# Five arrival slots and three split halves in place of four and four, in a one-core diffusion layer

## The chip, the cores and the metric

The kernel runs on one core of a Trainium2 chip. The metric is the device time of one launch in microseconds. Matrix products run on TensorE (PE), elementwise work on VectorE (DVE), ScalarE (ACT) and GpSimd (POOL); SyncE (SP) issues most of the transfers from memory (HBM).

## What is computed

One layer of a hybrid backbone over 256 latent tokens and 256 context tokens of width 2048, in fp32. Only the latent stream is an output. Cut to what matters:

```python
ul = (xl * (1 + sc1_l) + sh1_l) @ w_in          # combined projection, 2048 -> many columns
uc = (xc * (1 + sc1_c) + sh1_c) @ w_in
ya_c, ya_l = _hgrn_mixer(uc, ul, lb_fwd, lb_bwd, hgrn_norm, need_ctx)   # gated recurrence, two directions
yc_c, yc_l = _attention_mixer(uc, ul, attn_sink, need_ctx)
yb_l = _pool_mixer(ul, pool_w, pool_scale)
xl = _layer_norm(ALPHA * xl + g1_l * _merge_branches(ul, (ya_l, yb_l, yc_l), w_branch, w_out), ln1_g, ln1_b)
xl = _layer_norm(ALPHA * xl + g2_l * _sq_relu_mlp(xl * (1 + sc2_l) + sh2_l, w_ff1, w_ff2), ln2_g, ln2_b)
```

The shifts, scales and gates (`sh1`, `sc1`, `g1`, ...) come from `silu(c) @ w_ada + b_ada`. All weights together are some 370 chunks of 1 MB.

## The kernel before

**Chunks and slots.** Every weight is read in chunks of 512 input rows by 512 columns, as [128, 4, 512] fp32, 1 MB. `stream()` lists them in the order of use. SyncE issues one transfer per chunk into a ring of slots `raw0`, `raw1`, ...: eight slots while the first `w_ada` chunks are read (four of them, the `EXTRA` ones, lie in room that later tiles take), then `RAW` = 4. Before a transfer into a slot it waits until the chunk that held the slot is used up (L373 to L378): for a weight chunk until its second half has its low part (`lo_made`), for a summed chunk until its sum is done (`ada_used`).

**Split halves.** A product in fp32 is made of three matmuls: the weights are split into a high part `whi` (ScalarE's cast, L399) and a low part `wlo` (VectorE's subtraction, L842), the activations likewise, and TensorE adds hi*hi, hi*lo and lo*hi. One half chunk (two of the four row tiles) is split at a time. `whi` and `wlo` have four places, used in turn: half q goes to place q % 4, and ScalarE waits, before it casts half q, until TensorE has finished with half q-4 (L396 to L398; `w_used` and `blk_done` count TensorE's ends). VectorE waits for the cast (`hi_made`), TensorE for the low part (`lo_made`).

**Order by hand.** Each engine has its own program, written out in order. On ScalarE and VectorE the loops over chunks all have one form: `split_after(name, n)` converts both halves of the chunk after n, and then comes the engine's other work of this step, which TensorE wants after its matmuls of chunk n:

- vals, L431 to L455 and L914 on: keys and values; per weight chunk VectorE also sums two `w_ada` chunks (`ada_sum`, L856 to L864, four steps for a chunk).
- forget, four groups of four chunks: one sum per chunk, and a gate block (L926 to L953) of four scans and logs, whose keys ScalarE makes (L473) and TensorE turns at the end of the group (L1437).
- mix, two groups of twelve chunks: nine levels of the recurrence. GpSimd makes the exponents (L720 to L723), ScalarE the exponentials (L536), VectorE copies the scores of level k-1 (L988, L990) and multiplies the operands of the next (`lv`, L975), and TensorE makes the scores (L1483) after the chunk; then the outputs (L1494 to L1497).
- gates, branch 0: sixteen attention units. After each chunk TensorE makes one unit's scores (L1529) and turns another's probabilities (L1537). VectorE does a unit's mask, maximum and scaling (L1065 to L1078) behind the split.
- gates, branches 1 and 2, then the output projection (`out`), and the MLP in four parts of 16 + 16 chunks (`mlp`).

`features` (L1253 to L1255) keeps weights as the stationary operand and gives columns x tokens; a half is 24 matmuls of 256 or 512 columns. `tokens` (L1292 to L1294) gives tokens x columns for two tiles of 128 tokens (t = 0, 1); a half is 12 matmuls of 512 columns. For the last block of `out` and of `mlp` the last two chunks (`apart=2`) are gone through for tile 0 first and then for tile 1, so that tile 0's row work (`out_rows`, or `ff_out` and `last_rows`) begins while TensorE works on tile 1. All four places are held in this stretch.

Of the kernel before, what the change touches and what calls it, by code (L numbers as in the profile page):

```python
# [7 lines left out]
F32 = mybir.dt.float32  # L8
F32R = mybir.dt.float32r
# [5 lines left out]
P = 128  # L15
# [4 lines left out]
PW = 512  # L20
# [8 lines left out]
NEG = -1e30  # L29
WINDOWS = (2, 4, 8, 16)  # L30
LEVELS = (128, 64, 32, 16, 8, 4, 2, 1, 0)
RAW = 4

EXTRA = 4


PAN_AQ, PAN_AI, PAN_AG, PAN_AF, PAN_B, PAN_CQ, PAN_CKV, PAN_GATE = 0, 2, 4, 6, 10, 12, 14, 15
# [52 lines left out]
def stream():  # L90
# [14 lines left out]

    st.ring = RAW
    done = 0
# [96 lines left out]
PN = panels()  # L204


def build(nc, vecs, cst, rcnt, masks, xT, xtok, rows, w_ada, w_in, pool_w, w_br, w_out, w_f1, w_f2, outT):
    weights_of = {"w_ada": w_ada, "w_in": w_in, "w_br": w_br, "w_out": w_out, "w_f1": w_f1, "w_f2": w_f2}
    with ExitStack() as ctx:
        KB = 1024  # L210
# [4 lines left out]
        def at(name, shape, off, dt=F32):  # L215
            return nc.alloc_sbuf_tensor_at(name, shape, dt, offset=base + int(off))

        slots = [at(f"raw{n}", [P, CK, PW], off * KB)
                 for n, off in enumerate((0, 8, 16, 24, 160, 168, 184, 208))]
        whi = at("whi", [P, 4, 2, PW], 32 * KB, F32R)  # L220
        wlo = at("wlo", [P, 4, 2, PW], 48 * KB, F32R)

# [92 lines left out]
        hi_made, lo_made, ada_used, raw_used = sem("hi_made"), sem("lo_made"), sem("ada_used"), sem("raw_used")  # L317
# [69 lines left out]
        def _(act):  # L387
# [3 lines left out]
            def split(name, n, halves=(0, 1)):  # L391
                slot = ST.slot(name, n)
                act.wait_ge(raw_full[slot], ST.full(name, n))
                for h in halves:
                    q = ST.half(name, n, h)
                    if q >= 4:  # L396
                        which, count = PN.last[q - 4]
                        act.wait_ge(ended[which], count)  # L398
                    nc.scalar.copy(whi[:, q % 4], slots[slot][:, 2 * h:2 * h + 2]).then_inc(hi_made, 1)  # L399

            def split_after(name, n):
                if ST.following(name, n):
# [430 lines left out]
        def _(dve):  # L833
            TT, TS, STT = nc.vector.tensor_tensor, nc.vector.tensor_scalar, nc.vector.scalar_tensor_tensor
            drain = nc.vector.drain

            def split(name, n, halves=(0, 1)):
                slot = ST.slot(name, n)
                for h in halves:
                    q = ST.half(name, n, h)  # L840
                    dve.wait_ge(hi_made, q + 1)
                    TT(wlo[:, q % 4], slots[slot][:, 2 * h:2 * h + 2], whi[:, q % 4].bitcast(F32),  # L842
                       ALU.subtract).then_inc(lo_made, 1)

            def split_after(name, n):
# [393 lines left out]
        def _(pe):  # L1239
# [7 lines left out]
            def half_ready(name, n, h):  # L1247
                q = ST.half(name, n, h)
                pe.wait_ge(lo_made, q + 1)
                return q % 4  # L1250

            def three(out, w_hi, w_lo, x_hi, x_lo, start, stop):
                mm(out, w_hi, x_hi, start=start, stop=False)  # L1253
# [344 lines left out]

            for i in range(4):
                tokens("out", 4 * i, 4, 2 * (i % 2), mR, ready=lambda k: pe.wait_ge(m_lo, k + 1),  # L1600
                       between=lambda k: merged(3) if i == 0 and k == 0 else None, apart=2 if i == 3 else 0)

            def normalized(q, t):

# [14 lines left out]
            for f in range(4):  # L1619
                for i in range(4):  # L1620
                    def after(k):
                        if f == 0 and i == 0 and k < 2:
                            normalized(2 + k, 0)
                            normalized(2 + k, 1)
                    features("mlp", 32 * f + 4 * i, h2, 0, T, ready=lambda k, h: pe.wait_ge(h2_lo, 2 * k + h + 1),
                             between=after)
                for i in range(4):
                    tokens("mlp", 32 * f + 16 + 4 * i, 4, 2 * (i % 2), hid,
                           ready=lambda k: pe.wait_ge(hid_lo, 16 * f + 4 * k + 4),
                           between=lambda k: ada_spread(12 + f) if i == 0 and k == 0 else None,  # L1630
                           apart=2 if f == i == 3 else 0)


def constants():
# [65 lines left out]
```

## Time and profile before

| | us |
|---|---|
| median of 3 runs | 2015.3 |
| lowest, highest | 2012.96, 2015.35 |
| profiled execution, its own time | 2018.67 |
| its span | 2016.9 |
| TensorE busy | 1905.7 |
| VectorE busy | 1267.5 |
| ScalarE busy | 784.7 |
| GpSimd busy | 439.9 |

The mean granted clock of TensorE is 0.976 of full speed, and 409 MB move at a mean of 203 GB/s. Times inside the span are counted from its start. A row of the timeline gives start, length, engine, line, operation, tiles, a count of merged equal instructions, and in brackets the engine's idle time before it and what ended it. TensorE's matmuls overlap, so a matmul's own length is more than its share of the time.

### The profile page before, as it was taken

To read this page: it belongs to the slowest core of one execution; us is meant where nothing else is said; L and a number is where in the kernel's file an instruction comes from. 1 tells how busy PE (TensorE), PEld (TensorE's weight loads), DVE (VectorE), ACT (ScalarE), POOL (GpSimd) and SP (SyncE) were. 2 spreads that over 40 slices of the span, in tenths; PEclk is the share of its full clock that TensorE was granted. 3 is DMA by queue.
4 is the path that set the end of the run, shared out by engine and by line. 5 is a ranking of instruction groups with operands and counts; after the bars stand their busy time and mean duration, and the time that the engine had idled before them with its cause. 6 is when DMAs were issued, how large, how long until landed. Compare 5 with 4: busy or idle time off the path is not lost.

```text
span 2016.9 us, 26285 instructions
## 1 busy us (share of the span) xinstructions
PE 1905.7 (94%) x10808; PEld 1634.5 (81%) x10808; DVE 1267.5 (63%) x1419; ACT 784.7 (39%) x898; POOL 439.9 (22%) x335
## 2 busy tenths in 40 slices
PE   6899899999898989999999999999999999999996
PEld 1478787889888867777778887997899899889975
DVE  1345656785666575667867666767566556556686
ACT  1221224454544545544344444533333333333332
POOL 0000000003727322023421000246045005302510
PEclk8999999999999999999999999899999999999998
DMA  9956554454333244456666674465665556656552
GB/s 401 421 199 225 215 197 175 169 188 168 105 126 111 98 159 144 147 173 265 229 234 248 263 257 167 185 242 179 229 230 218 200 209 223 212 192 225 217 180 89
DMA packets 59320, 409.05 MB, mean 203 GB/s; under 512 B 6336, under 2 KB 9024, under 8 KB 10304
## 3 DMA queue, kind: packets, MB, share of 16 engines
q1 hardware_dynamic: 54720, 395.34, 53.4%
q10 hardware_dynamic: 4480, 12.02, 1.6%
q8 instruction: 86, 1.41, 0.3%
q14 instruction: 34, 0.28, 0.0%
HBM read 405.24 MB, written 2.10 MB: 202 GB/s over the span
## 4 chain that ended last, share of the span: by engine, by line
PE 71%; DVE 13%; DMA 4%; DVEq 3%; issue 3%; POOL 3%; ACT 2%; POOLq 0%; SPq 0%; ACTq 0%
PE main L1292 12%; PE main L1294 12%; PE main L1293 12%; PE main L1253 9%; PE main L1254 9%; PE main L1255 9%; DVE asum L863 5%; DVE wlo L842 4%; DMA raw<-in_w_in 2%; DVEq L862 2%; DMA raw<-in_w_ada 2%; PE side L1324 1%; ACT whi L399 1%; PE side L1483 1%; PE main L1343 1%
## 5 line engine op out<-in xcount | busy, mean ns | idle before, releaser
L842 DVE TENSOR_TENSOR wlo<-raw,whi 128x1024 fp32r<-128x1024 f32 x552 | 742.4, 1372 | 414.3 <-ACT whi L399 413.8
L399 ACT CAST whi<-raw 128x1024 fp32r<-128x1024 f32 x552 | 571.8, 1050 | 854.6 <-PE main L1294 349.1
L1253 PE MATMUL main<-h,whi 128*128 128x256 f32 x1024 | 291.4, 285 | 4.1 <-DVE h L1160 2.1
L1254 PE MATMUL main<-h,whi 128*128 128x256 f32 x1024 | 291.0, 284 | 0.0
L1255 PE MATMUL main<-h,wlo 128*128 128x256 f32 x1024 | 290.9, 284 | 0.0
L1253 PE MATMUL main<-hCL,whi 128*128 128x256 f32 (+1 forms) x800 | 264.6, 331 | 14.0 <-DVE wlo L842 3.8
L1254 PE MATMUL main<-hCL,whi 128*128 128x256 f32 (+1 forms) x800 | 260.5, 326 | 0.0
L1255 PE MATMUL main<-hCL,wlo 128*128 128x256 f32 (+1 forms) x800 | 260.2, 325 | 0.0
L863 DVE SCALAR_TENSOR_TENSOR asum<-raw,sm,asum 128x512 f32<-128x512 f32 x240 | 200.9, 837 | 19.7 <-issue 0.9
L1292 PE MATMUL main<-whi,hid 128*128 128x512 f32 x512 | 201.9, 394 | 5.1 <-DVE wlo L842 4.4
L1253 PEld LDWEIGHTS main<-h,whi 128*128 128x128 f32 x1024 | 197.9, 193 | 4.8 <-DVE h L1160 2.5
L1293 PE MATMUL main<-wlo,hid 128*128 128x512 f32 x512 | 200.0, 391 | 0.0
L1294 PE MATMUL main<-whi,hid 128*128 128x512 f32 x512 | 199.9, 390 | 0.0
L1254 PEld LDWEIGHTS main<-h,whi 128*128 128x128 f32 x1024 | 197.8, 193 | 0.1
L1255 PEld LDWEIGHTS main<-h,wlo 128*128 128x128 f32 x1024 | 197.8, 193 | 0.0
L823 POOL TENSOR_TENSOR sq<-sq 128x256 f32<-128x256 f32 x64 | 66.2, 1035 | 521.1 <-DVE sq L1169 513.4
L1253 PEld LDWEIGHTS main<-hCL,whi 128*128 128x128 f32 x800 | 155.3, 194 | 27.3 <-DVE wlo L842 10.8
L1255 PEld LDWEIGHTS main<-hCL,wlo 128*128 128x128 f32 x800 | 154.7, 193 | 11.9
L1254 PEld LDWEIGHTS main<-hCL,whi 128*128 128x128 f32 x800 | 155.0, 194 | 11.4 <-issue 0.2
L1292 PE MATMUL main<-whi,hCL 128*128 128x512 f32 x384 | 155.6, 405 | 8.8 <-DVE wlo L842 8.8
L1293 PE MATMUL main<-wlo,hCL 128*128 128x512 f32 x384 | 150.7, 393 | 0.0
L1294 PE MATMUL main<-whi,hCL 128*128 128x512 f32 x384 | 150.7, 392 | 0.0
(229 smaller groups left out, 2674.3 us busy)
## 6 DMA issues: line engine op xcount, KB each, us to landing
raw<-in_w_f SPq DMA_DIRECT2D x128, 1024.0 KB, 5.0
raw<-in_w_in SPq DMA_DIRECT2D x108, 1024.0 KB, 5.0
raw<-in_w_ada SPq DMA_DIRECT2D x96, 1024.0 KB, 7.0
raw<-in_w_br SPq DMA_DIRECT2D x24, 1024.0 KB, 6.9
raw<-in_w_out SPq DMA_DIRECT2D x16, 1024.0 KB, 5.0
xin<-in_xT SPq DMA_DIRECT2D x4, 1024.0 KB, 19.9
ax<-in_xtok ACTq DMA_DIRECT2D x1, 2048.0 KB, 8.0
lng<-in_rows ACTq DMA_DIRECT2D x2, 1024.0 KB, 5.8
```

The costliest lines, as they stand in the source:

```text
L399: nc.scalar.copy(whi[:, q % 4], slots[slot][:, 2 * h:2 * h + 2]).then_inc(hi_made, 1)
L823: TT(sq[:, b], sq[:, b], sq[:, b], ALU.mult)
L842: TT(wlo[:, q % 4], slots[slot][:, 2 * h:2 * h + 2], whi[:, q % 4].bitcast(F32), ALU.subtract).then_inc(lo_made, 1)
L862: drain()
L863: last = STT(asum[:], slots[slot][:, j], s, asum[:], ALU.mult, ALU.add)
L1253: mm(out, w_hi, x_hi, start=start, stop=False)
L1254: mm(out, w_hi, x_lo, start=False, stop=False)
L1255: return mm(out, w_lo, x_hi, start=False, stop=stop)
L1292: mm(out, x[:, kt, 0, own], whi[:, par, j], start=start, stop=False)
L1293: mm(out, x[:, kt, 0, own], wlo[:, par, j], start=False, stop=False)
L1294: last = mm(out, x[:, kt, 1, own], whi[:, par, j], start=False, stop=stop)
L1324: last = mm(side[group, 1 + p % 2], sR[:, k * CK + j], slots[slot][:, j], start=k == 0, stop=k == 3, tile_position=(0, 32 * j), skip_group ...
```

## The change

The ring has five slots after the first stage in place of four; the early stage has eight in both (5 + 3). The split halves have three places in place of four, so ScalarE's cast of half q waits for TensorE's end of half q-3. The fifth slot takes the 8 KB that the two fourth places gave up. The last block of `out` and of `mlp` keeps one chunk apart in place of two.

```diff
-RAW = 4
-
-EXTRA = 4
+RAW = 5
+
+HALVES = 3
+
+EXTRA = 3
...
         slots = [at(f"raw{n}", [P, CK, PW], off * KB)
-                 for n, off in enumerate((0, 8, 16, 24, 160, 168, 184, 208))]
-        whi = at("whi", [P, 4, 2, PW], 32 * KB, F32R)
-        wlo = at("wlo", [P, 4, 2, PW], 48 * KB, F32R)
+                 for n, off in enumerate((0, 8, 16, 24, 32, 160, 168, 184))]
+        whi = at("whi", [P, HALVES, 2, PW], 40 * KB, F32R)
+        wlo = at("wlo", [P, HALVES, 2, PW], 52 * KB, F32R)
...
                     q = ST.half(name, n, h)
-                    if q >= 4:
-                        which, count = PN.last[q - 4]
+                    if q >= HALVES:
+                        which, count = PN.last[q - HALVES]
                         act.wait_ge(ended[which], count)
-                    nc.scalar.copy(whi[:, q % 4], slots[slot][:, 2 * h:2 * h + 2]).then_inc(hi_made, 1)
+                    nc.scalar.copy(whi[:, q % HALVES], slots[slot][:, 2 * h:2 * h + 2]).then_inc(hi_made, 1)
...
-                    TT(wlo[:, q % 4], slots[slot][:, 2 * h:2 * h + 2], whi[:, q % 4].bitcast(F32),
+                    TT(wlo[:, q % HALVES], slots[slot][:, 2 * h:2 * h + 2], whi[:, q % HALVES].bitcast(F32),
...
-                return q % 4
+                return q % HALVES
...
-                       between=lambda k: merged(3) if i == 0 and k == 0 else None, apart=2 if i == 3 else 0)
+                       between=lambda k: merged(3) if i == 0 and k == 0 else None, apart=1 if i == 3 else 0)
...
-                           apart=2 if f == i == 3 else 0)
+                           apart=1 if f == i == 3 else 0)
```

What this moves in the engines' programs. SyncE, in the stage of keys and values, where two `w_ada` chunks stand between two `w_in` chunks; in brackets is the count that the transfer waits for. Before:

```order
47 L379 DMA raw2_51<-in_w_in 128x2048 [waits ada_used]
48 L379 DMA raw3_52<-in_w_ada 128x2048 [waits lo_made]
49 L379 DMA raw0_49<-in_w_ada 128x2048 [waits ada_used]
50 L379 DMA raw1_50<-in_w_in 128x2048 [waits ada_used]
51 L379 DMA raw2_51<-in_w_ada 128x2048 [waits lo_made]
```

And of the changed kernel, the same five transfers:

```order
47 L381 DMA raw2_51<-in_w_in 128x2048 [waits ada_used]
48 L381 DMA raw3_52<-in_w_ada 128x2048 [waits ada_used]
49 L381 DMA raw4_53<-in_w_ada 128x2048 [waits lo_made]
50 L381 DMA raw0_49<-in_w_in 128x2048 [waits ada_used]
51 L381 DMA raw1_50<-in_w_ada 128x2048 [waits ada_used]
```

The order of the transfers is the same, but a `w_in` chunk now takes the slot of the first of the two sums before it, and the wait for the second sum (`ada_used`) has moved to the `w_ada` chunk behind it.

TensorE, in the last four half chunks of the MLP, the first matmul of each run of six (one half, one tile); `hid_lo` marks where the last chunk is begun for tile 0. Before:

```order
9939 L1292 MATMUL main<-whi_57,hid_89 128x512 [waits lo_made]
...
9945 L1292 MATMUL main<-whi_57,hid_89 128x512 [waits lo_made,hid_lo]
...
9951 L1292 MATMUL main<-whi_57,hid_89 128x512 [waits lo_made]
...
9957 L1292 MATMUL main<-whi_57,hid_89 128x512 [waits lo_made]
...
9963 L1292 MATMUL main<-whi_57,hid_89 128x512 [waits lo_made]
```

And of the changed kernel:

```order
9939 L1294 MATMUL main<-whi_57,hid_89 128x512 [waits lo_made]
...
9945 L1294 MATMUL main<-whi_57,hid_89 128x512 [waits lo_made]
...
9951 L1294 MATMUL main<-whi_57,hid_89 128x512 [waits lo_made]
...
9957 L1294 MATMUL main<-whi_57,hid_89 128x512 [waits lo_made,hid_lo]
...
9963 L1294 MATMUL main<-whi_57,hid_89 128x512 [waits lo_made]
```

Before, tile 0 enters the last chunk two runs earlier and is done with it at row 9956, ahead of four runs for tile 1; now it is done at row 9968, ahead of two. The order of ScalarE's, VectorE's and GpSimd's instructions is unchanged; what the casts wait for is not.

## Rows read from the trace of the kernel before

**Rows 1.** The page, shares of the chain that ended last, by engine.

```profile
PE 71%; DVE 13%; DMA 4%; DVEq 3%; issue 3%; POOL 3%; ACT 2%; POOLq 0%; SPq 0%; ACTq 0%
```

**Rows 2.** TensorE's waits, whole span: waiting line <- releaser: us, times, longest.

```profile
PE side L1483 <- DVE lv L975: 18.8, 10, 3.5
...
PE side L1437 <- ACT kctx L473: 4.4, 3, 2.6
```

**Rows 3.** ScalarE's waits, whole span.

```profile
ACT whi L399 <- PE main L1294: 349.1, 213, 6.0
ACT whi L399 <- PE main L1255: 303.7, 156, 9.4
ACT whi L399 <- DMA raw<-in_w_in: 192.1, 31, 13.1
```

**Rows 4.** Stretches: length, busy PE, PEld, DVE, ACT, POOL, then clock, DMA share, GB/s.

```profile
173.00:251.00 78.00, 67.67 (x368) 58.69 (x368) 46.17 (x56) 17.78 (x22) 0.00 (x0) 0.91 0.58 213
...
480.00:694.00 214.00, 191.01 (x1463) 185.72 (x1462) 135.18 (x125) 99.46 (x95) 105.80 (x66) 0.96 0.35 121
694.00:887.00 193.00, 183.79 (x809) 145.30 (x809) 122.78 (x182) 102.72 (x151) 44.36 (x20) 0.97 0.41 139
```

**Rows 5.** Timeline of ScalarE where keys and values are projected.

```profile
173.44 1.99 ACT L399 CAST whi<-raw 128x1024 fp32r<-128x1024 f32 x2 [12.66 <-DMA raw<-in_w_in]
...
188.39 2.01 ACT L399 CAST whi<-raw 128x1024 fp32r<-128x1024 f32 x2 [11.01 <-DMA raw<-in_w_in]
```

**Rows 6.** Timelines of ScalarE, VectorE and TensorE around one attention unit.

```profile
751.46 1.05 ACT L399 CAST whi<-raw 128x1024 fp32r<-128x1024 f32 x1 [1.62 <-PE main L1294]
...
752.14 2.35 DVE L842 TENSOR_TENSOR wlo<-raw,whi 128x1024 fp32r<-128x1024 f32 x2
...
755.31 0.69 DVE L1068 TENSOR_REDUCE col<-side 128x1 f32<-128x512 f32 x1 [0.43 <-issue]
...
758.02 0.49 DVE L1078 TENSOR_SCALAR pr<-pr,col 128x512 f32<-128x512 f32 x1
...
758.04 1.02 PE L1529 MATMUL side<-ak,qr 128*128 128x512 f32 x2
758.90 0.60 PE L1537 MATMUL side<-cs,pr 128*128 128x128 f32 x4
```

**Rows 7.** Timelines of ScalarE, VectorE and TensorE among the recurrence levels.

```profile
569.10 1.04 ACT L399 CAST whi<-raw 128x1024 fp32r<-128x1024 f32 x1 [1.78 <-PE main L1255]
...
487.74 1.22 DVE L975 TENSOR_TENSOR lv<-lv,q_t 128x1024 f32<-128x1024 f32 x1
...
519.65 3.44 DVE L842 TENSOR_TENSOR wlo<-raw,whi 128x1024 fp32r<-128x1024 f32 x2 [1.38 <-ACT whi L399]
...
524.46 2.11 DVE L975 TENSOR_TENSOR lv<-lv,q_t 128x1024 f32<-128x1024 f32 x1
...
526.62 2.05 PE L1483 MATMUL side<-lv 128*128 128x128 f32 x16 [0.48 <-DVE lv L975]
```

**Rows 8.** Timelines of ScalarE, VectorE and TensorE around one turn of the keys.

```profile
356.30 1.06 ACT L399 CAST whi<-raw 128x1024 fp32r<-128x1024 f32 x1 [1.29 <-PE main L1255]
...
367.18 1.06 ACT L399 CAST whi<-raw 128x1024 fp32r<-128x1024 f32 x1 [2.92 <-PE main L1255]
...
368.68 2.35 DVE L842 TENSOR_TENSOR wlo<-raw,whi 128x1024 fp32r<-128x1024 f32 x2
371.13 3.24 DVE L863 SCALAR_TENSOR_TENSOR asum<-raw,sm,asum 128x512 f32<-128x512 f32 x4
...
378.55 1.10 PE L1437 MATMUL side<-cs,kctx 128*128 128x128 f32 x8 [0.53 <-ACT kctx L473]
```

**Rows 9.** TensorE's waits between 870 and 1170 us.

```profile
PE main L1292 <- DVE wlo L842: 8.8, 7, 2.5
```

**Rows 10.** Timeline of VectorE at the end, the first rows of either token tile.

```profile
1994.97 0.69 DVE L1180 TENSOR_TENSOR res<-main,g2b 128x512 f32<-128x512 f32 x1 [3.20 <-PE main L1294]
...
2004.68 0.68 DVE L1180 TENSOR_TENSOR res<-main,g2b 128x512 f32<-128x512 f32 x1
```

## The prediction

> **What bounds the kernel now.** I read the chain that ended last first: TensorE's own work is 71% of the span, VectorE's 13%, DMA 4% [rows 1]. So TensorE sets the time, and everything else costs only what TensorE waits for. Then I read TensorE's waits by releaser. The largest group is the level scores of the recurrence, released by VectorE's `lv` product, 18.8 us; the turned keys are 4.4 us [rows 2], and between 870 and 1170 us the low parts `wlo` of the weights are 8.8 us [rows 9]. Third, ScalarE's waits: it sat idle before the cast `whi` for 349.1 and 303.7 us until TensorE had finished with a half chunk, and for 192.1 us until a chunk had landed [rows 3]. These two kinds of wait are what the change moves: it buys arrival room (a fifth slot) with conversion room (a fourth half). Neither kind of wait is on the path by itself. The question is at each place what is queued behind it. Last I read the stages: in 173 to 251 us TensorE is idle 78 - 67.7 = 10.3 us at a clock of 0.91, in 480 to 694 us 23.0 us at 0.96, in 694 to 887 us 9.2 us at 0.97 [rows 4].
>
> **The fifth slot.** It pays where two `w_ada` chunks are summed per weight chunk. There the casts start at 173.44 and 188.39 us, both the moment a chunk lands, and so on at this pace for five chunks [rows 5]. One turn is 14.95 us: transfer, two casts, two `wlo`, two sums, and only then the next transfer's slot is free. In the new order of SyncE a weight chunk waits for the first sum, not for the second. A sum of one chunk is 3.24 us [rows 8], so the turn falls to 11.7 us. TensorE's 67.7 us of work for the five chunks of this stretch, at a clock of 0.91 [rows 4], are 67.7 x 0.91 / 5 = 12.3 us a chunk at full speed, so TensorE sets the pace again. What goes is the 10.3 us of idle time and, with the waits, most of what the low clock costs, 78 x 0.09 = 7 us at most. Gain: 15 us, between 8 and 17. Elsewhere ScalarE's waits for a landing are not followed by a wait of TensorE of any size, so I give the slot nothing more.
>
> **The missing half.** Cast q now waits for TensorE's end of half q-3 instead of q-4. ScalarE and VectorE always convert both halves of the following chunk ahead of their other work. With four halves, the second half of chunk k+1 was cast when chunk k began. Now it is cast when the first half of chunk k ends, one half later. Where VectorE has nothing to do but this, it is free: a cast is 1.05 us, a `wlo` 2.35 / 2 = 1.2 us, with hand-overs 2.4 us from the release to the ready pair, and TensorE comes two halves later, over 5.2 us (the time between two releases of ScalarE, its idle time and the cast before it, is TensorE's half: 1.62 + 1.05 = 2.67 us with tokens [rows 6], 1.78 + 1.04 = 2.82 us with 256 columns [rows 7]). That covers the MLP and the output projection. Where work that TensorE needs at the end of chunk k stands behind this `wlo`, it is not covered. Three stages have that form.
>
> *Attention*, 16 units. Behind the `wlo` pair stand the mask, maximum, exponential's sum and scaling of a unit: pair 752.14 to 754.49, scaling done at 758.02 + 0.49 = 758.51, so 4.0 us after the pair, 3.6 us without this unit's own pause of 0.43 us; TensorE turns the result at 758.90 [rows 6]. New: the pair ready 2.4 us after the release, then 3.6 us and a hand-over, 6.1 us after the first half's end. TensorE has 2.67 us of matmuls and 758.90 - 758.04 = 0.86 us of the next scores in that time. It waits 2.6 us per unit, and 3.4 us in the last two of eight, which have no scores to issue. That is 2 x (6 x 2.6 + 2 x 3.4) = 45 us; about 5 of the 9.2 us idle there now [rows 4] are the same waits. Cost 40 us. Bounds: 30, if in some units VectorE is late anyway and the cast's lateness costs nothing, and 50, with the pause in each.
>
> *Recurrence levels*, 18. Behind the pair (519.65 to 523.09) stand two copies and the product of the next level, done at 524.46 + 2.11 = 526.57; TensorE starts at 526.62 [rows 7], 3.5 us after the pair. The same product takes 1.22 us elsewhere [rows 7], so 2.6 us is the other end. New: 2.4 + 2.6 to 3.5 us after the first half's end, against 2.82 us of matmuls: 2.2 to 3.1 us per level, 2.6 taken. The first level of each group has no copies (0.8 us), and the inter-chunk output behind it has two exponentials and two products (about 3.7 us). That is 2 x (0.8 + 8 x 2.6 + 3.7) = 50.6 us, in place of today's 18.8 us [rows 2], since a level that waits for the split is no longer waiting for GpSimd. Cost 32 us, bounds 22 and 40.
>
> *Forget gates*, three turns of keys. The second cast was released at 367.18, VectorE took its pair at 368.68 to 371.03, and TensorE got the keys at 378.55, 7.5 us later, behind a sum and a gate block [rows 8]. One half of 512 columns is (367.18 - 356.30) / 2 = 5.4 us. In the new order the release is one half later, at 372.6; the pair ends at 374.95 and the keys come at 382.5: 3.9 us later. TensorE's matmuls end 0.53 us before the keys come today, so it would wait 4.4 us. Three turns of 4.4 us against 4.4 us in all today [rows 2]: cost 9 us, between 6 and 11.
>
> *Second branch*, 887 to 1031 us. Here `wlo` ends just as TensorE needs it (8.8 us of waits [rows 9]), behind a sum. At three places the later cast pushes the pair by 2 us: cost 6 us, between 0 and 10.
>
> **Ends apart.** The last token block lets its first 128 tokens finish early. With one chunk apart in place of two, the first tile ends one half's time later, 2.67 us. VectorE's work on it begins at 1994.97 and runs without a gap into the second tile's at 2004.68 [rows 10], so VectorE is the path there and the end moves by all of it: 2.7 us. At the output projection the same happens ahead of the norm: 2.7 us. A few places of the MLP (residual rows on VectorE and GpSimd) add 4 us, between 0 and 6. Cost 9.4 us.
>
> **The clock.** Each wait costs more than itself: the granted clock is 0.91, 0.96 and 0.97 in the three stretches [rows 4], short spells at 1.2 GHz around the longer waits. Time lost so is at most 78 x 0.09 = 7 us on 10.3 us of idle time, 214 x 0.04 = 9 us on 23.0 us, 193 x 0.03 = 6 us on 9.2 us, so 0.4 to 0.7 us per us idle; a part of a spell falls into the wait itself and costs nothing. The terms above add 87 us of waits and take 10 away. I take 0.35 of 77, 27 us, between 0 and 0.6 of it, 46 us.
>
> **Sum.** -15 + 40 + 32 + 9 + 6 + 9.4 + 27 = +108 us. The profiled execution took 2018.7 us and the median is 2015.3 us; both contain the same waits, so I add it to the median: 2124 us.
>
> **A rule weighed.** The rows show TensorE two halves away from the half that ScalarE casts, and VectorE with 4 us of other work in between. The Trainium skill (Trainium Kernel Development and Optimization, Best Practices) asks to double-buffer so that transfers overlap compute. By that rule three halves, and five slots, are plenty: only the gain in transfers and the two tails would be seen, which is the first rival.
>
> **Rivals.** (1) *Faster: the cover holds.* If ScalarE's and VectorE's lateness stays inside the conversion room, only the slot's gain and the ends remain: -15 + 5.4, about 2006 us. It decides if what stands behind the pair is under 0.3 us (2.7 - 2.4). The rows show 4.0, 3.5 and 7.5 us [rows 6 to 8], and TensorE already starts within 0.4 us of VectorE in the first two. Chance 0.03. (2) *The waits come, the clock stays.* 2015.3 + 81 = 2097 us. For it speaks that most new waits are under 3 us; against it that the attention now loses 6 us of clock on waits of the same size. Chance 0.22. (3) *The clock falls behind nearly every new wait, and `wlo` collides more with GpSimd*: 2150 us and more, chance 0.13. (4) *The slot does nothing*, because the third sum's transfer queues ahead of the weight chunk: +15 us, 2140 us, chance 0.05. (5) Gains and losses cancel: 0.02. The forecast itself has 0.55.
>
> **Numbers.** 2124 us; the range 2088 to 2160 takes in rival 2 and most of rival 3. About 0.2% is what a measurement can tell from no change: faster 0.03, same 0.02, slower 0.95.
>
> **What would show it.** TensorE's waits for `lv` near 50 us, for `pr` or the attention's products near 45 us, for `kctx` near 13 us; waits in 173 to 235 us gone and ScalarE's casts there every 11.5 us; ScalarE's wait for a landing under 192.1 us; granted clock under 0.95 in 480 to 900 us; the last part of the page's busy row unchanged but 2.7 us longer. I am wrong if the level scores still wait under 25 us, or if the casts of second halves are released by TensorE without its waiting afterwards.

## The result

The changed kernel took 2142.9 us (median of four runs, 2140.2 to 2149.5), against 2015.3 for the kernel before; the ratio is 1.0605, 95% interval 1.0568 to 1.0642. In a later group of runs the same two kernels gave 2146.4 and 2018.4, ratio 1.0621 (1.0591 to 1.0652). The change makes the kernel slower by 6%. Ratios leave out one execution, in the run with the shorter distance alone, that took 6614.3 us. In the code of the changed kernel everything behind the first edit stands two lines lower: L1483 is now L1485, L1529 is L1531, L842 is L844, and so on; in the experiments the rows have each run's own line numbers, and the tile names tell which line is meant.

**The path.** Of the changed kernel, the page's shares of the chain that ended last [before: rows 1]:

```profile
PE 77%; DVE 11%; issue 4%; ACT 4%; DMA 2%; DVEq 1%; POOL 1%; POOLq 0%; ACTq 0%; SPq 0%
```

TensorE still sets the time, and has the same 10808 matmuls. The span rose from 2016.9 to 2142.5 us. It must be looked for in what TensorE waits for, and in the rate at which it works.

**TensorE's waits**, whole span of the changed kernel (waiting line, releaser, us, times, longest), to be held against [rows 2] and [rows 9]:

```profile
PE side L1485 <- DVE lv L977: 37.9, 16, 3.7
PE side L1531 <- ACT col L591: 28.5, 12, 2.7
...
PE side L1539 <- DVE pr L1080: 16.5, 4, 6.4
PE side L1439 <- ACT kctx L475: 13.5, 3, 4.6
PE side L1531 <- POOL ak L758: 6.5, 1, 6.5
PE side L1496 <- issue: 6.5, 2, 3.2
PE side L1485 <- DVE lv L979: 4.1, 2, 2.1
```

The level scores wait 37.9 + 4.1 us where it was 18.8, the keys 13.5 where it was 4.4, and the attention (scores L1531, transposes L1539) waits 28.5 + 16.5 + 6.5 = 51.5 us in 17 places, where the kernel before waited 9.2 us in three. ScalarE's waits, beside [rows 3]:

```profile
ACT whi L401 <- PE main L1296: 545.9, 269, 9.2
ACT whi L401 <- PE main L1257: 506.7, 190, 13.8
ACT whi L401 <- DMA raw<-in_w_in: 68.7, 8, 9.8
```

This is the exchange in three rows: ScalarE waits 123 us less for chunks to land (192.1 to 68.7) and 400 us more for TensorE to give a place back (349.1 + 303.7 to 1052.6).

**Stretches** of the changed kernel, columns as in [rows 4]: the start, the late part of keys and values, forget and query, the recurrence (482 to 742), the attention (742 to 985), the second branch.

```profile
0.00:173.00 173.00, 145.80 (x710) 88.38 (x711) 63.18 (x102) 38.11 (x52) 1.66 (x6) 0.93 0.85 340
173.00:251.00 78.00, 78.00 (x447) 68.75 (x446) 50.47 (x61) 18.53 (x20) 0.00 (x0) 1.00 0.71 257
...
300.00:480.00 180.00, 164.17 (x916) 145.19 (x915) 113.73 (x174) 76.18 (x110) 5.09 (x4) 0.93 0.44 158
...
482.00:742.00 260.00, 211.38 (x1509) 203.67 (x1510) 121.26 (x130) 103.32 (x97) 94.70 (x70) 0.91 0.29 98
742.00:985.00 243.00, 191.53 (x740) 144.05 (x739) 112.45 (x177) 96.72 (x147) 33.38 (x17) 0.90 0.33 111
...
985.00:1170.00 185.00, 170.34 (x720) 137.62 (x719) 132.69 (x109) 68.85 (x75) 63.59 (x35) 0.97 0.61 228
```

And of the kernel before, its recurrence (480 to 699) and its attention (699 to 882), the same work as in the fourth and fifth row above:

```profile
480.00:699.00 219.00, 196.01 (x1505) 190.72 (x1504) 136.32 (x128) 104.11 (x100) 107.01 (x67) 0.96 0.34 118
699.00:882.00 183.00, 173.79 (x746) 136.16 (x745) 116.64 (x178) 96.09 (x144) 38.41 (x18) 0.97 0.43 147
```

The second row shows the gain: in 173 to 251 us TensorE has no idle time at all and the full clock, where it had 10.3 us and 0.91 [rows 4]. The fourth and fifth row show the loss: 49 and 51 us without work where it was 23 and 9, and a clock of 0.91 and 0.90 where it was 0.96 and 0.97.

Taken by the end of the last half of each stage, the difference to before is (us; a stage's own length, after minus before):

| stage | length before | difference |
|---|---|---|
| up to the eighth values chunk | 173.2 | +0.4 |
| values 8 to forget 1 | 87.4 | -17.8 |
| forget 2 to 15 | 165.3 | +9.4 |
| query | 53.8 | +10.1 |
| recurrence levels | 219.7 | +40.3 |
| attention | 182.5 | +61.0 |
| second branch | 140.1 | +9.6 |
| third branch and projection | 235.0 | -0.7 |
| MLP, first quarter | 201.5 | +6.9 |
| MLP, the rest | 541.8 | +3.8 |
| behind TensorE's last half | 16.6 | +2.7 |

The differences add up to 125.7, the spans differ by 125.6. TensorE's idle gaps of over 0.25 us are 94.2 us in all before and 176.5 after, 82 us more. The mean clock of 0.976 over 2016.9 us is 48 us of lost time, 0.958 over 2142.5 us is 90: 42 us more. These two make up the loss. The mean clock counts low spells inside the waits too, so as a check without it: the same 10808 matmuls keep TensorE busy for 1946.3 us in place of 1905.7, 40.6 us more, and it is without work for 196.2 us in place of 111.2, the end behind its last half included.

**One attention unit** of the changed kernel, timelines of ScalarE, VectorE and TensorE [before: rows 6]:

```profile
788.17 1.05 ACT L401 CAST whi<-raw 128x1024 fp32r<-128x1024 f32 x1 [1.18 <-PE main L1296]
...
792.20 0.69 ACT L588 ACTIVATE pr<-side,col 128x512 f32<-128x512 f32 x1 [1.19 <-DVE col L1074]
...
789.26 1.23 DVE L844 TENSOR_TENSOR wlo<-raw,whi 128x1024 fp32r<-128x1024 f32 x1 [1.01 <-ACT whi L401]
790.58 0.30 DVE L1067 TENSOR_TENSOR side<-side,cs 128x128 f32<-128x128 f32 x1
...
772.67 1.84 PE L1531 MATMUL side<-ak,qr 128*128 128x512 f32 x2 [2.25 <-ACT col L591]
...
790.24 0.39 PE L1295 MATMUL main<-wlo,yR 128*128 128x512 f32 x1
...
793.21 1.91 PE L1531 MATMUL side<-ak,qr 128*128 128x512 f32 x2 [2.36 <-ACT col L591]
```

To be read in this order: the cast of the second half cannot begin before 788.17, when TensorE has ended the first half of the running chunk. VectorE stands idle 1.01 us for it, makes the low part, and only at 790.58 turns to the mask and the maximum of a unit whose scores have lain ready for 16 us: in step k VectorE works on unit k-2, and this unit's scores were made at 772.67 and done at 774.5. TensorE's own matmuls end at about 790.85. The exponential (792.20) is 1.6 us behind the mask. TensorE's next scores go into the bank that this exponential reads, so it goes on at 793.21, after 2.36 us. Such a wait of 2.35 or 2.36 us stands ten times in the stage.

### The profile page after: what moved, and what is told of

Read it like the earlier page. It is cut to its first block, busy times and chain, and to the rows that moved or that the text cites. A ratio compares the mean times of both kernels' runs of the same rounds, so it can differ in the third digit from the quotient of the medians.

```text
span 2142.5 us, 26285 instructions
## 1 busy us (share of the span) xinstructions
PE 1946.3 (91%) x10808; PEld 1661.1 (78%) x10808; DVE 1237.6 (58%) x1419; ACT 788.3 (37%) x898; POOL 418.9 (20%) x335
## 3 DMA queue, kind: packets, MB, share of 16 engines
q1 hardware_dynamic: 54720, 395.34, 50.6%
## 4 chain that ended last, share of the span: by engine, by line
PE 77%; DVE 11%; issue 4%; ACT 4%; DMA 2%; DVEq 1%; POOL 1%; POOLq 0%; ACTq 0%; SPq 0%
PE main L1294 11%; PE main L1295 11%; PE main L1296 11%; PE main L1255 10%; PE main L1256 10%; PE main L1257 10%; DVE wlo L844 4%; ACT whi L401 2%; PE side L1485 2%; DMA raw<-in_w_ada 2%; DVE asum L865 2%; PE main L1345 2%; PE main L1347 1%; PE main L1346 1%; PE side L1326 1%
## 5 line engine op out<-in xcount | busy, mean ns | idle before, releaser
L844 DVE TENSOR_TENSOR wlo<-raw,whi 128x1024 fp32r<-128x1024 f32 x552 | 734.8, 1340 | 728.4 <-ACT whi L401 728.2
L401 ACT CAST whi<-raw 128x1024 fp32r<-128x1024 f32 x552 | 578.6, 1051 | 1135.1 <-PE main L1296 545.9
L865 DVE SCALAR_TENSOR_TENSOR asum<-raw,sm,asum 128x512 f32<-128x512 f32 x240 | 195.3, 814 | 19.7 <-issue 0.9
L1294 PE MATMUL main<-whi,hCL 128*128 128x512 f32 x384 | 159.4, 415 | 14.7 <-DVE wlo L844 14.7
L1255 PEld LDWEIGHTS main<-hCL,whi 128*128 128x128 f32 x800 | 157.7, 197 | 14.5 <-DVE wlo L844 2.7
L1256 PEld LDWEIGHTS main<-hCL,whi 128*128 128x128 f32 x800 | 157.0, 196 | 11.4 <-issue 0.2
L1296 PE MATMUL main<-whi,hCL 128*128 128x512 f32 x384 | 153.0, 398 | 0.0
L825 POOL TENSOR_TENSOR sq<-sq 128x256 f32<-128x256 f32 x64 | 40.1, 626 | 535.9 <-DVE sq L1171 528.2
```

The source lines that it names most:

```text
L401: nc.scalar.copy(whi[:, q % HALVES], slots[slot][:, 2 * h:2 * h + 2]).then_inc(hi_made, 1)
L825: TT(sq[:, b], sq[:, b], sq[:, b], ALU.mult)
L844: TT(wlo[:, q % HALVES], slots[slot][:, 2 * h:2 * h + 2], whi[:, q % HALVES].bitcast(F32), ALU.subtract).then_inc(lo_made, 1)
L865: last = STT(asum[:], slots[slot][:, j], s, asum[:], ALU.mult, ALU.add)
L1256: mm(out, w_hi, x_lo, start=False, stop=False)
L1294: mm(out, x[:, kt, 0, own], whi[:, par, j], start=start, stop=False)
```

## The experiments

Times in brackets are those of the kernel before in the same group of runs.

### The ring set back to four slots

```diff
-RAW = 5
+RAW = 4
-EXTRA = 3
+EXTRA = 4
```

> The changed kernel with the ring of arriving chunks set back to four slots (and the fourth slot for the MLP stages kept, so that four are extra in place of three). Three halves and the shorter distance at the end stay. Theory: the fifth slot alone ended the loading waits of 11 us in the values stage, so they come back between 173 and 260 us, and no other stage changes: the stretch from the fifth values chunk to the second forget chunk is 17 to 18 us longer again, the span 2158 to 2161. Rival (the slot did nothing; the loading waits went for another reason, because conversions now sit nearer to the arrivals): the time stays at 2143 within 2, and no wait of 11 us at the first matmul of a half comes back.

2171.5 us (2017.3), ratio 1.0762 (1.0738 to 1.0786). The window and the casts of this kernel:

```profile
173.00:251.00 78.00, 67.03 (x364) 58.02 (x362) 43.74 (x55) 15.15 (x19) 0.00 (x0) 0.91 0.58 209
...
181.39 1.99 ACT L401 CAST whi<-raw 128x1024 fp32r<-128x1024 f32 x2 [12.66 <-DMA raw<-in_w_in]
196.21 2.00 ACT L401 CAST whi<-raw 128x1024 fp32r<-128x1024 f32 x2 [10.88 <-DMA raw<-in_w_in]
```

The idle 11 us, the clock of 0.91 and the casts 14.8 us apart are back, as in [rows 4] and [rows 5]. The stretch from values 8 to forget 1 is 88.0 us long, against 69.5 with five slots and 87.4 before; all later stages agree with the changed kernel within 1.1 us. So the slot is worth its 18 us even with three halves, and nothing elsewhere. The time rose by more, 25 to 29 us, and the span is 2167.7 where I had written 2158 to 2161: up to the eighth values chunk the profiled execution of this kernel took 180.9 us, 7.3 more than that of the changed one. The last experiment shows how much this start scatters. But all four executions of this kernel lie between 2169.5 and 2172.0 us, and only one was profiled, so that the whole excess is chance isn't shown.

### The shorter distance alone

```diff
-  apart=2 if i == 3 else 0)          # last block of the output projection
+  apart=1 if i == 3 else 0)
-  apart=2 if f == i == 3 else 0)     # last block of the MLP
+  apart=1 if f == i == 3 else 0)
```

> The kernel before with one edit: the last token tiles of the second projection stage and of the MLP end apart over one chunk, not two. Four slots and four halves stay. Theory: the last tile's last eight matmuls of 256 columns (0.17 us each) no longer lie behind tile 3's own finish, so VectorE's last reductions begin later at both places: 2.7 at the end of the kernel, about 2.7 at the join before the MLP, so 2020 to 2021. The same after VectorE's last reduction (19 us of tail in place of 16.6) should show. Rival (the distance matters only with three halves): 2015 within 1.

2024.8 us (2017.3), the median of all twelve executions, 2023.3 without the long one; ratio 1.0035 (1.0019 to 1.0051), so 4 to 10 us more; I had written 2020 to 2021. The reason that I had given does not fit the code: no matmul of 256 columns is in question, and no row has 0.17 us for one; the edit moves two runs of six matmuls of 512 columns, one half's time. By stages (of the profiled execution, the longest of the other eleven, which also lost 5.2 us in the start): +3.2 in the MLP's first features, +3.0 in its first tokens, +2.7 behind TensorE's last half. VectorE's first row of either tile at the end, beside [rows 10]:

```profile
2008.77 0.69 DVE L1180 TENSOR_TENSOR res<-main,g2b 128x512 f32<-128x512 f32 x1 [5.92 <-PE main L1294]
...
2018.47 0.68 DVE L1180 TENSOR_TENSOR res<-main,g2b 128x512 f32<-128x512 f32 x1
```

TensorE's last half ended at 2011.4, so the second tile's row work began 7.1 us behind it; in the kernel before it was 2004.68 against 2000.3, 4.4 us. Both ends cost what a half costs. The 3.0 us in the MLP's first tokens I had not expected. TensorE waits there for a `wlo` that GpSimd holds up. First two stretches of the kernel before, then the same two, 8 us later, of this one:

```profile
1392.00:1398.00 6.00, 4.61 (x12) 3.16 (x12) 6.00 (x4) 0.56 (x1) 5.16 (x1) 0.72 0.53 175
1398.00:1406.00 8.00, 7.61 (x34) 6.34 (x35) 5.66 (x6) 2.59 (x3) 0.00 (x0) 1.00 0.69 261
```

```profile
1400.00:1406.00 6.00, 3.04 (x12) 2.17 (x12) 6.00 (x4) 1.04 (x1) 5.30 (x1) 0.99 0.51 175
1406.00:1414.00 8.00, 7.47 (x20) 5.93 (x21) 4.63 (x5) 1.05 (x1) 0.00 (x0) 0.58 0.68 251
```

Before, the low clock (0.72) fell on twelve matmuls behind which TensorE waited for VectorE anyway, and cost nothing. Here the same twelve ran at 0.99, TensorE waited longer, and the low clock (0.58) fell on the work after the wait: 8 x 0.42 = 3.4 us of lost time. Why it fell later by this much I can't say. Three halves and a distance of two could not be tried together, since the distance of two holds four halves at once.

### The second conversion behind the attention's work

```diff
 # ScalarE and VectorE, attention stage, step k
-split_after("gates", 12 * h + k)               # both halves of the next chunk
+split_after("gates", 12 * h + k, (0,))         # its first half
 ...                                            # the unit's softmax work
+split_after("gates", 12 * h + k, (1,))         # its second half
```

> The changed kernel (three halves), with one move in the attention stage alone: ScalarE and VectorE convert the first half of the next chunk ahead of the unit's softmax work, as now, but the second half behind it. Theory: the waits of TensorE at the scores, at the transposes and at the rotated keys are there because the softmax work is queued behind a conversion that waits for TensorE to finish a half; with that conversion behind, the stage (705 to 985 in the changed kernel) gives back its 61 us, or all but some 6 to 10: the kernel 2143 to 2085 or 2093, the clock about 0.97, and 28.5 us of score waits and 16.5 of transpose waits fall below 10 together. The recurrence levels, 40 us, stay as they are. Rival A (three halves are too few whatever the order: conversions are late themselves): the score waits go, but waits of the same length stand at the first matmul of a half, and the time stays above 2130. Rival B (the stage is slow for the clock, not for the waits): waits go and low clock stays, 2110 to 2120.

2077.4 us (2017.3), ratio 1.0299 (1.0270 to 1.0328): 65 to 69 us less than with the change alone. The attention's two halves are -1.6 and -0.1 us against before, so all of the 61 us is back, with three halves; I had expected 2085 or more. The waits that are left there, and the stretch of this kernel's attention:

```profile
PE side L1533 <- POOL ak L759: 5.7, 1, 5.7
...
PE side L1541 <- DVE pr L1081: 2.5, 1, 2.5
...
PE side L1533 <- ACT col L591: 1.0, 2, 0.8
...
747.00:927.00 180.00, 170.75 (x740) 133.50 (x739) 114.90 (x176) 97.25 (x146) 37.80 (x18) 0.98 0.44 149
```

28.5 us of score waits are 1.0, 16.5 of transpose waits are 2.5, and the clock went from 0.90 to 0.98 with them. Rival A is out: no waits at first matmuls took their place. The recurrence kept its +40.2.

### The same in the other stages

```diff
 # forget, query, levels: as above; on ScalarE's levels only at k == 10
-split_after("mix", 12 * i + k)
+split_after("mix", 12 * i + k, (0,) if k == 10 else (0, 1))     # ScalarE
-split_after("mix", 12 * i + k)
+split_after("mix", 12 * i + k, (0,))                            # VectorE
 ...                                                             # operands of level k
+split_after("mix", 12 * i + k, (1,))
```

> The changed kernel with the move of the attention run carried to the other stages with work behind the conversions: in forget, query, the recurrence levels (mix) and attention, the second half of the next chunk is converted behind the stage's own work on VectorE, and on ScalarE too except in the first levels, where only the place ahead of the outputs is moved. Theory: all waits but the last 7 of the gates stage came from the order of the queues, so forget gives back 9, query some 8 of 10, and mix some 38 of 40; with attention's 61: from 2143 to 2024 to 2032; waits at the levels (37.9) fall below 20 and at the keys (13.5) below 5. Rival A (three halves are short by themselves in mix, where TensorE's chunks are short): the level waits turn into waits at first matmuls of a half, mix stays 20 or more longer than before, 2045 to 2060. Rival B (the level's work on ScalarE, not VectorE, is late): the mix stage stays at +40, about 2060.

2005.5 us (2018.4), ratio 0.9940 (0.9917 to 0.9963). That is 18.5 us better than the best value I had written, and faster than the kernel before, with three halves; the slot's 17.8 us are in it. Forget is -0.1 us against before, query 0.0, the recurrence -12.9, the attention -1.7, the second branch still +3.6, the MLP +11.1.

```profile
PE side L1493 <- DVE lv L983: 4.7, 8, 1.1
...
460.00:667.00 207.00, 192.21 (x1510) 186.50 (x1511) 135.11 (x130) 103.99 (x98) 109.79 (x70) 0.98 0.36 123
```

The row to look at is the first: it was 37.9 in the changed kernel and 18.8 in the kernel before. I had counted on the state of before as the floor; but of the 18.8 us that stood there some 14 came from the same queue. In the levels VectorE's order is enough: ScalarE still casts both halves ahead there.

### Only VectorE's order, in the attention

```diff
 # VectorE only; ScalarE converts both halves ahead, as in the changed kernel
-split_after("gates", 12 * h + k)
+split_after("gates", 12 * h + k, (0,))
 ...
+split_after("gates", 12 * h + k, (1,))
```

> The changed kernel with the move of the attention run on VectorE alone: there the second half's correction comes behind the unit's softmax work, while ScalarE keeps both conversions ahead of it. Theory: the scores wait for ScalarE, whose softmax steps are queued behind a conversion that waits for TensorE's last half, so VectorE's order gives back little: TensorE's waits at the scores stay within 5 of 28.5, the attention stage stays 45 to 65 longer than before, and the time is 2130 to 2150. VectorE's corrections may come late now and add a few us. Rival (VectorE's correction of the second half was what held up the softmax, as it does the recurrence levels): the stage falls to within 20 of before and the time to about 2100.

2096.6 us (2018.6), ratio 1.0398 (1.0364 to 1.0433). My theory fell and the rival held: the stage is +15.0 us against before, not +45 to +65.

```profile
PE side L1540 <- DVE pr L1080: 9.3, 4, 6.4
...
PE side L1532 <- ACT col L591: 4.3, 5, 1.2
```

I had read the releaser of the long row, ScalarE's `col`, as the cause. It is only the last link: ScalarE's exponential waits for the maximum (`DVE col L1074` in the unit's timeline above), and it was VectorE that stood behind the conversion. Its order alone gives back 46 of the 61 us. With ScalarE's too, as in the run above, it is 63, 1.7 us better than before. ScalarE's order alone can't be tried: its exponential would wait for a maximum that VectorE makes behind the second half, and that half's cast would stand behind the exponential.

### The clock by itself

```diff
+if u >= 3:
+    pe.wait_ge(at_cp, h * 8 + u - 2)
+    for _ in range(16):
+        mm(side[:, 2, 0:T], hCL[:, 0, 0, C:C + P], hCL[:, 0, 0, C:], start=True, stop=True)
 if u >= 2:
     pe.wait_ge(at_exp, h * 8 + u - 1)          # and then the scores
```

> The changed kernel with 16 matmuls of 256 columns added ahead of each wait for the scores in attention (units 3 to 7 of each half), into a bank of the side accumulators that is free there; nobody reads what they write. They fill most of a wait of 2.35 (16 x 0.107 is 1.7) and make nothing that is waited for earlier or later, so they measure the clock's part by itself. Theory: of attention's 61 some 43 is waits and some 20 is TensorE at the lower clock behind them; filled waits leave no low clock behind the scores, the stage (742 to 985) falls by 10 to 15 and the kernel to 2128 to 2133; granted clock of 705 to 985 goes from 0.90 to about 0.95. Rival (the clock falls whatever TensorE does between, or the low clock lies inside waits): the stage keeps its length or grows by up to 17, the clock stays at 0.90.

2134.0 us (2018.4), ratio 1.0586 (1.0556 to 1.0617), beside 1.0621 for the changed kernel in the same group; 1 us above what I had expected, and the intervals overlap, so the stages must speak. TensorE's timeline around one unit, its score waits, and the attention's stretch:

```profile
785.64 2.07 PE L1532 MATMUL side<-hCL 128*128 128x256 f32 x16
788.16 1.12 PE L1535 MATMUL side<-ak,qr 128*128 128x512 f32 x2 [0.44 <-ACT col L591]
...
PE side L1535 <- ACT col L591: 9.5, 12, 2.4
...
742.00:985.00 243.00, 207.68 (x926) 163.37 (x924) 121.41 (x178) 97.44 (x146) 43.13 (x22) 0.94 0.34 115
```

The two stretches of 50 us in which all filled waits lie, of this kernel and then of the changed one:

```profile
775.00:825.00 50.00, 47.43 (x242) 37.86 (x241) 23.84 (x47) 20.23 (x36) 0.00 (x0) 1.00 0.40 137
889.00:939.00 50.00, 47.77 (x243) 38.12 (x243) 23.37 (x47) 21.35 (x36) 0.00 (x0) 1.00 0.32 106
```

```profile
780.00:830.00 50.00, 38.04 (x142) 27.53 (x141) 21.87 (x43) 19.10 (x35) 0.00 (x0) 0.90 0.37 123
900.00:950.00 50.00, 38.22 (x151) 27.65 (x150) 22.95 (x46) 19.82 (x34) 0.00 (x0) 0.94 0.31 106
```

A wait of 2.36 us is now 2.07 us of matmuls and 0.44 us of wait, so nothing moves but the clock. The attention is 8.4 us shorter (I had expected 10 to 15), its clock 0.94 in place of 0.90. TensorE does more work in the stage and finishes it sooner. In the whole stage TensorE's clock fell twelve times in the changed kernel and six times here, never at a filled wait. That is direct evidence that the clock is a price of its own. Ten waits were filled, nine of them of 2.35 or 2.36 us and one of 2.68; 2.07 + 0.44 is 0.15 us more than 2.36, so the matmuls added 1.5 us and the clock gave back 8.4 + 1.5 = 9.9, or 0.4 us for each of the 23.9 us of wait. The five waits at transposes and rotated keys, most of them longer, and the first two at scores were not filled. The rest of the run's gain, 5.5 us in the recurrence, is no effect of the edit, which lies behind it; there the clock came out better for a reason that no run shows. The run with only VectorE's order has the same 4 us less in the first group of the recurrence.

### The slot alone

```diff
+    st.names = (0, 1, 2, 3, 8)       # from the fifth values chunk; slot 8 lies on bytes still unused
 for n in range(16):
+    if n == 2:
+        st.names = (0, 1, 2, 3)      # from the third forget chunk, as before
     panel("forget", n, 0, "w_in", 4 * PAN_AF + n)
```

Four halves and the distance of two stay.

> The kernel before, with the fifth slot alone: four halves and the old distance at the end stay, and the fifth slot lies on bytes that hold nothing yet between the fifth values chunk and the second forget chunk; from there on the ring has four slots again. Theory: the gain of the slot (17.8 us between 173 and 260) stands by itself and needs none of the other parts; its loading waits of 11 us go, all later stages are as before: 1997 to 2000, ratio 0.991 to 0.993. Rival (the gain in that stretch of the changed kernel came with three halves, not with the slot): 2015 within 2. Second rival (the loads that come sooner make the ring empty later, at the switch back to four): some 4 to 8 of the gain stands again as waits in the forget stage, 2004 to 2010.

2000.4 us (2017.3), ratio 0.9920 (0.9896 to 0.9944): faster than the kernel before. Its window is that of the changed kernel:

```profile
173.00:251.00 78.00, 78.00 (x447) 68.75 (x446) 52.71 (x65) 20.19 (x23) 0.00 (x0) 1.00 0.68 247
```

Values 8 to forget 1 is -17.8 us, the same as in the changed kernel to a tenth, and no later stage gives any of it back. The slot pays within these 70 us. It holds its 8 KB for 111 us, from the first transfer into it (issued at 114.3) to the end of its last sum (225.3), while the bytes of a later tile lie idle.

### The slot and the order, with four halves

The edits of "The slot alone" and of "The same in the other stages" on the kernel before.

> The kernel before (four halves, four slots from the second forget chunk on, distance two) with the fifth slot in the early stages, as in the run with the slot alone, and the same moves of the second half's conversion in forget, query, mix and attention. Theory: with four halves half of the waits at the levels (18.7), at the keys (4.4) and at the scores and rotated keys (7) are left from the same queues, so part of them goes with their clock: 1985 to 1995 where the slot alone gave 2000. Rival (with four halves the conversion ahead does not wait for TensorE there, so its place behind only makes the next chunk's halves later): 2000 or above, with new waits at first matmuls of a half.

1979.8 us (2018.4), ratio 0.9811 (0.9786 to 0.9836), the best of all and 5 us below what I had written. Its waits at the levels, and its recurrence:

```profile
PE side L1493 <- DVE lv L983: 4.8, 4, 1.6
...
471.00:673.00 202.00, 189.99 (x1512) 185.47 (x1511) 132.02 (x129) 105.20 (x101) 104.71 (x67) 0.99 0.38 129
```

18.2 us less in the recurrence than before and 8.1 less in the attention, of which the run with the slot alone, whose order there is the old one, already has 3.2. With the order right, the fourth half is still worth something: the run with three halves in the same order loses 5.3 us to this one in the recurrence, 6.4 in the attention, 2.7 in the second branch and some 14 in the MLP and at the end, where the shorter distance is part of it.

### The changed kernel again

> The changed kernel itself again, unaltered, as the yardstick of this group of runs: 2143, and the stages before 173 us tell how much a run's start scatters (the first eight chunks ended between 173.2 and 181.0 in kernels that do the same thing up to there).

2146.4 us (2018.4). From the eighth values chunk on every stage agrees with the first profile within 0.2 us. Only the start differs, 181.2 against 173.7 us. Its first stretch, beside the first row of the stretches of the changed kernel:

```profile
0.00:173.00 173.00, 145.94 (x677) 86.96 (x678) 58.58 (x97) 34.46 (x47) 1.66 (x6) 0.85 0.80 323
```

TensorE is busy for the same 146 us, but at a clock of 0.85 in place of 0.93, and does 677 matmuls in place of 710. Over the whole stage it is without work for 27.2 and 27.1 us, and busy for 146.5 and 154.2. So what scatters from one execution to the next (over all kernels this stage ended between 171.3 and 182.5 us, with 26.9 to 29.4 us without work) is the clock in the start, not the waits for weights. Why the clock differs there, no run shows. In the profiled execution of the run with four slots the 7.3 us are of this kind: 5.1 of them are busy time.

## Why the prediction was right, and where it was not

The forecast was 2124.0 us, the range 2088 to 2160, and the time 2142.9. The direction, the mechanism and the stages were right; the time lies 19 us above the forecast, and rival 4 (2140 us), which came out nearest by its number, is refuted by the runs on the slot.

- **The fifth slot**: -15 predicted, -17.8 measured, the upper bound of 17 just passed. The reading was right: the turn of 14.95 us is gone, and TensorE, busy for all of 173 to 251 us, sets the pace. That pace I had put too slow, at 12.3 us a chunk, by sharing 78 us among five chunks where 5.2 turns fit; and the gain was reckoned for 78 us of a stage of 87.4. Six chunks now take 69.5 us, 11.6 each, and the casts came at 179.69, 190.98 and 202.75 us, every 11.5, as ScalarE's timeline of the changed kernel shows:

```profile
179.69 2.00 ACT L401 CAST whi<-raw 128x1024 fp32r<-128x1024 f32 x2 [5.41 <-DMA raw<-in_w_in]
190.98 2.00 ACT L401 CAST whi<-raw 128x1024 fp32r<-128x1024 f32 x2 [9.30 <-DMA raw<-in_w_in]
202.75 2.00 ACT L401 CAST whi<-raw 128x1024 fp32r<-128x1024 f32 x2 [9.77 <-DMA raw<-in_w_in]
```

Both runs on the slot give the same 18 us.
- **Attention**: the place was right, the waiting row one matmul off. I expected TensorE at the turned probabilities; it stands before the scores, which wait for the exponential of the unit before and come first in its program. The waits are 28.5 + 16.5 + 6.5 = 51.5 us where 45 were predicted, 2.36 us per unit where I had 2.6, and 3.35 us in three of the four last units where I had 3.4. The difference is in the first half: a wait of 6.5 us for GpSimd's rotated keys, which I had not listed, and 6.4 us in place of 3.4 in the seventh unit.
- **Recurrence levels**: 50.6 us of waits predicted, 37.9 + 4.1 + 6.5 = 48.5 found. Single waits lie between 2.0 and 3.7 us, but for one of 0.7, predicted 2.2 to 3.1.
- **Keys**: three waits of 4.4 us predicted, 13.5 us in three found. Forget and query together are 19.5 us longer, where the term was 9: I had not listed a wait of 2.1 us for `q_t` in query, and the clock's share, 0.93 in 300 to 480 us, was far above what 0.35 per us of wait gives.
- **Second branch**: +6 predicted, +9.6 measured, of which 6.1 is idle time; the rest is the clock (0.97 where it was 0.99).
- **Ends**: 9.4 predicted. 2.7 at the end was exact, 3.7 at the join stands for 2.7, and the MLP's 4 us became 7.0 (3.2 in its first tokens, 3.8 later). The run with the distance alone shows that most of the first part belongs to the distance, not to the missing half.
- **The clock**: the step that failed in size. Sum of the waits: 87 less 10 predicted, and 6.7 us of the ends that TensorE waits out, 84 in all; 82 found. The clock's own loss was put at 27 us, less some 5 that leave with the slot, 22 us net, and is 42 (48 to 90 us over the span; 40.6 by the busy time). My own rows said 0.4 to 0.7 us for each us idle; I took 0.35, with the argument that a part of each low spell falls into the wait. What was found is 42 / 82 = 0.51. The run with filled waits gives 0.4 for waits of 2.4 us. Taking the middle of my rows, 0.55 x 77 = 42, would have put the forecast at 2139.
- **The rule weighed**: the Trainium skill (Trainium Kernel Development and Optimization, Best Practices) asks to double-buffer so that DMA overlaps compute. Read as a rule for the halves too, it would call three plenty: some 2006 us, and the kernel took 2142.9. With the second conversion behind the other work it took 2005.5. That the two numbers meet is luck: recurrence and attention came out 14.6 us below the kernel before, the second branch and the MLP 14.7 above it. Three halves cost little where nothing that TensorE needs is queued behind the conversion that waits for it, but not nothing: four in the same order took 1979.8.

Rival 1 is refuted as the change stands; with the order changed only its number came. Rival 2 (clock unchanged, 2097) is refuted by the clock rows; rival 3 (2150 and more) has the right tendency, as the clock fell behind most waits, though not behind all.

## What to carry to other kernels

A buffer more for one thing and a buffer less for another must be priced by what stands behind the waiting instruction: on an engine that works in program order, a conversion ahead whose place comes free late holds up everything written after it, here 100 us, although ScalarE is busy for 37% of the span and VectorE for 58%. Before giving up or adding a buffer, write the instruction that waits behind the urgent work; here that was worth 141 us with three halves (2146.4 to 2005.5) and 21 with four (2000.4 to 1979.8). And look where memory is free for a short time only: the slot pays in 70 us of 2000 and holds its bytes for 111, and there they cost nothing.

## What the hardware showed

- TensorE's clock fell to its low level, 1.2 GHz, around most of the new waits, short ones too: around 12 of the 17 in the attention, and around five of the ten of 2.35 or 2.36 us. The mean over the recurrence is 0.91 where it was 0.96, over the attention 0.90 where it was 0.97. Sixteen matmuls that nobody reads, in each of ten waits, left no low spell at any of them, brought the attention back to 0.94 and shortened it by 8.4 us.
- Whether a low spell costs anything depends on where it falls: on matmuls ahead of a wait for another engine it was free (0.72 in 1392 to 1398 us of the kernel before), behind the wait it was paid (0.58 in 1406 to 1414 us with the shorter distance, in a stage 3.0 us longer).
- The execution-to-execution scatter of this kernel sits in its first 173 us, as a clock between 0.85 and 0.93 for the same work. Later stages repeat within 0.2 us in the two profiles of the changed kernel. Between kernels they can differ with no edit in them: the recurrence by 5.5 us in the run with filled waits and by 3.8 with VectorE's order alone, the attention by 3.2 in the run with the slot alone.
- VectorE's low part of 1.2 us takes 4.8 to 5.6 us beside GpSimd's wide operations. VectorE and GpSimd of the kernel before, in the MLP's first quarter:

```profile
1376.87 15.88 DVE L842 TENSOR_TENSOR wlo<-raw,whi 128x1024 fp32r<-128x1024 f32 x3 [1.45 <-ACT whi L399]
...
1380.74 5.41 POOL L815 TENSOR_TENSOR ax<-ax,lnb 128x2048 f32<-128x2048 f32 x1
```

Three low parts took 15.88 us while GpSimd ran four operations of 4.6 to 5.6 us without a break, and each low part ended 1.1 us after one of the operations did. That is a third thing, beside ring and halves, that decides how far ahead a conversion must stand; no run here separates it. The Trainium skill (SBUF — State Buffer, on who interferes with whom) calls the port pair that the two engines share an exclusive lock; these rows agree with it, since a low part waits an operation out instead of running beside it.
